# Waits and order of the transposes in a linear-attention stage of a two-block transformer

## The chip, the cores and the metric

The kernel runs as one program on one core of a Trainium2 chip. The metric is the device time of one execution in microseconds (us). The numbers below come from three timed runs and one profiled execution of the kernel before. Engines are called by their short names: PE (TensorE, matmuls and transposes), PEld (its weight loads), ACT (ScalarE), DVE (VectorE), POOL (GpSimd), SP (SyncE, which issues the loads).

## The reference, cut to what matters

Two transformer blocks run one after the other on 512 tokens of width 1024. The second block's mixer is gated linear attention with 4 heads, key width 128 and value width 256, run forward and backward over chunks of 64 tokens. Only that mixer is touched. Its core:

```
def gla_chunked(q, k, v, log_a, s0):
    q = q * (K ** -0.5)
    b = jnp.cumsum(log_a, axis=3)
    b_mid = b[:, :, :, CHUNK // 2 - 1:CHUNK // 2, :]
    b_last = b[:, :, :, CHUNK - 1:, :]
    scores = jnp.einsum('bhnik,bhnjk->bhnij', q * jnp.exp(b - b_mid), k * jnp.exp(b_mid - b))
    scores = jnp.where(causal, scores, 0.0)
    o_intra = jnp.einsum('bhnij,bhnjv->bhniv', scores, v)
    kv = jnp.einsum('bhnjk,bhnjv->nbhkv', k * jnp.exp(b_last - b), v)
    decay = jnp.moveaxis(jnp.exp(b_last[:, :, :, 0, :]), 2, 0)
    s_final, s_before = lax.scan(step, s0, (decay, kv))      # s <- decay * s + kv
    o_inter = jnp.einsum('bhnik,nbhkv->bhniv', q * jnp.exp(b), s_before)
    return o_intra + o_inter, s_final

o = rmsnorm(o, g_head)            # per head, over its 256 values
y_gla = (o * jax.nn.silu(g)) @ w_gla_out
```

log_a is log_sigmoid of a low-rank projection z plus a bias, divided by 16. The inputs q, k, v, g are products of the normed tokens with one wide matrix.

## The kernel before

Every fp32 product is made from three matmuls on split operands (high x high, low x high, high x low). A **tile** is one column block of 128 outputs for all 512 tokens: 8 k-blocks x 3 matmuls of 128x512 (line 1921), into PSUM bank G[0] or G[1]. Its weights pass through raw (DMA), whi (ACT, `high_part`, line 462) and wlo (DVE, `low_part`, line 468), two buffers of each.

The linear attention stage is in `gla_pe`, `gla_act` and `gla_dve`. It walks over eight **units** u = 0 to 7: head h = u // 2, direction r = u % 2. In the gaps between the attention's matmuls PE works on the tiles m, m+1, m+2 of the next head (or, from tile 24 on, of the convolution), in half tiles of 12 matmuls. No scheduler is at work: each engine runs its instructions in the order in which these functions write them, and semaphores (`g_...`) hold them back.

What happens in a unit:

- `z(u+1)` writes the next unit's decay logits into PSUM bank X[3]. ACT's `decay` reads the bank (Abs, then Exp and Ln, lines 2480 to 2484, semaphore g_ln), then DVE's `decay` reads it once (line 2606) and goes on in SBUF: subtract (701), scan (2611 or 2613), two differences and a copy, and then raises g_sums (line 2623). ACT's `exps` turns that into five exponentials, DVE's `factors` multiplies them by k and q and raises g_ke.
- `scores(u)` writes X[2]; DVE's `mask(u)` (2642) copies it under the causal mask into Am; `intra(u)` multiplies it by the values into the output banks AD and MS.
- `outer(u, n)` for n = 0 to 3 makes the k v products of two chunks in X[0] and X[1]; DVE's `states(u, n)` (2657) adds them to the running state and raises g_kv_taken, without which `outer(u, n+1)` waits; `inter(u, n)` multiplies the state by q.
- **Turns** are groups of four 128x128 transposes into the same bank X[3]: `turn_v` (the next head's values, in units with r = 1, two halves, 2352), `turn_o` (the previous head's output, in units with r = 0 and h > 0, two halves, 2374) and `turn_ke` (at the end of each unit, 2363). ACT copies v and ke out (2503, 2499). For the output, ACT's `scale_o` takes the mean square and scales AD and MS into oN (2535 to 2540, semaphore g_on), the turn follows, DVE's `gate_o` (2663) multiplies it by the gate into tb[3], ACT's `high` (2545) and DVE's `low_o` (2668) split it.

Since X[3] is shared, a turn may only write it when the decay's logits have been read. Before, the first `turn_v` and the first `turn_o` of a unit wait for g_sums, which comes at the end of DVE's `decay`.

`conv(n)` is four DVE operations on the convolution (2678 to 2689) for the odd tiles from 25 on, so in units 6 and 7 only.

Of the kernel before, what the change touches and what calls it, by code (L numbers as in the profile page):

```python
# [136 lines left out]
def program(nc, A, out, scr):  # L137
# [3 lines left out]
    def S(name):  # L141
        if name not in sems:
            sems[name] = ctx.enter_context(nc.semaphore(name))
        return sems[name]
# [4 lines left out]
    with ctx:  # L149
# [2173 lines left out]
        def gla_pe(E):  # L2323
            p = E.eng

            def tile(n, lo=0, hi=KD, parts=False):
                j = n % 2
                if lo == 0:
                    E.eng.wait_ge(S(f"free_G{j}"), USE0["hd"] + n // 2 + 1)
                    E.eng.wait_ge(S("w_split"), TILE0["hd"] + n + 3)  # L2330
                for kk in range(lo, hi):
                    if parts:
                        E.eng.wait_ge(S("part_ready"), E.nth("part_ready"))
                    mm = three(E, j, G[j][:, :], Ahi, Alo, kk, kk == 0, kk == KD - 1)
                if hi == KD:
                    mm.then_inc(S("tile_done"), 1)
# [7 lines left out]

            def turn_v(h, half):
                if half == 0:
                    E.eng.wait_ge(S("g_sums"), 1 if h == 0 else 2 * h + 1)
                else:
                    E.eng.wait_ge(S("g_v_copied"), 2 * h + 1)
                E.eng.wait_ge(S("g_v"), 2 * h + half + 1)  # L2350
                for b in range(4):
                    mm = p.transpose(X[3][:, b * P:(b + 1) * P], vT[:, half, b * P:(b + 1) * P], ident)
                mm.then_inc(S("g_v_turned"), 1)
# [12 lines left out]
            def turn_o(h, half):  # L2366
                if half == 0:
                    E.eng.wait_ge(S("g_on"), h + 1)
                    if h < GH - 1:
                        E.eng.wait_ge(S("g_sums"), 2 * h + 4)  # L2370
                else:
                    E.eng.wait_ge(S("g_o_taken"), 2 * h + 1)
                for b in range(4):
                    mm = p.transpose(X[3][:, b * P:(b + 1) * P], oN[:, b, half * P:(half + 1) * P], ident)
                mm.then_inc(S("g_o_turned"), 1)
# [60 lines left out]
            for u in range(NU):  # L2436
                h, r = u // 2, u % 2
                m = 6 * (h + 1) + 3 * r
                tile(m, 0, 4)
                if u + 1 < NU:  # L2440
                    z(u + 1)
                tile(m, 4, KD)
                if r == 0 and h > 0:
                    turn_o(h - 1, 0)
                scores(u)
                if r == 1 and h + 1 < GH:
                    turn_v(h + 1, 0)
                outer(u, 0)
                tile(m + 1, 0, 4)
                intra(u)  # L2450
                if r == 0 and h > 0:
                    turn_o(h - 1, 1)
                if r == 1 and h + 1 < GH:
                    turn_v(h + 1, 1)
                outer(u, 1)
                inter(u, 0)
                tile(m + 1, 4, KD)
                outer(u, 2)
                inter(u, 1)
                tile(m + 2, 0, 4)  # L2460
                outer(u, 3)
                inter(u, 2)
                tile(m + 2, 4, KD)
                inter(u, 3)
                if u + 1 < NU:
                    turn_ke(u + 1)
# [7 lines left out]
        def gla_act(E):  # L2474
# [90 lines left out]
            for u in range(NU):  # L2565
                h, r = u // 2, u % 2
                m = 6 * (h + 1) + 3 * r
                if u + 1 < NU:
                    decay(u + 1)
                if r == 0 and h > 0:  # L2570
                    scale_o(h - 1)
                take(m)
                if u + 1 < NU:
                    exps(u + 1)
                if r == 0 and h > 0:
                    high(h - 1, 0)
                    high(h - 1, 1)
                if r == 1 and h + 1 < GH:
                    copy_v(h + 1, 0)
                    copy_v(h + 1, 1)  # L2580
                take(m + 1)
                take(m + 2)
                if r == 1 and h + 1 < GH:
                    log_exp(E)
                if u + 1 < NU:
                    copy_ke(u + 1)
# [8 lines left out]
        def gla_dve(E):  # L2595
# [7 lines left out]
            def decay(u):  # L2603
                h, r = u // 2, u % 2
                E.eng.wait_ge(S("g_ln"), u + 1)
                v.tensor_scalar(tb[1][:, :], X[3][:, :], vec[:, V_BDEC + 4 * r + h:V_BDEC + 4 * r + h + 1], 0.0,
                                ALU.add, ALU.min)
                v.drain()
                each(E, (tb[1][:, :], tb[1][:, :], tb[0][:, :], ALU.subtract))
                if r == 0:  # L2610
                    v.tensor_tensor_scan(tb[2][:, :], con[:, C_CF:C_CF + T], tb[1][:, :], 0.0, ALU.mult, ALU.add)
                else:
                    v.tensor_tensor_scan(tb[2][:, ::-1], con[:, C_CB:C_CB + T][:, ::-1], tb[1][:, ::-1], 0.0,
                                         ALU.mult, ALU.add)
                v.drain()
                mid, end = (31, 63) if r == 0 else (32, 0)
                sh = [P, 8, CHUNK]
                v.tensor_tensor(tb[1].rearrange("p (c t) -> p c t", t=CHUNK),
                                b3[:, :, end:end + 1].to_broadcast(sh), b3, ALU.subtract)
                v.tensor_tensor(tb[0].rearrange("p (c t) -> p c t", t=CHUNK), b3,  # L2620
                                b3[:, :, mid:mid + 1].to_broadcast(sh), ALU.subtract)
                v.tensor_copy(dsum[:, :], b3[:, :, end])
                v.drain().then_inc(S("g_sums"), 1)
# [78 lines left out]
            for u in range(NU):  # L2702
                h, r = u // 2, u % 2
                m = 6 * (h + 1) + 3 * r
                if u + 1 < NU:
                    decay(u + 1)
                low(m)
                conv(m)
                if r == 0 and h > 0:
                    gate_o(h - 1, 0)  # L2710
                mask(u)
                states(u, 0)
                if u + 1 < NU:
                    factors(u + 1)
                if r == 0 and h > 0:
                    low_o(h - 1, 0)
                    gate_o(h - 1, 1)
                states(u, 1)
                if r == 0 and h > 0:
                    low_o(h - 1, 1)  # L2720
                low(m + 1)
                conv(m + 1)
                states(u, 2)
                states(u, 3)
                low(m + 2)
                conv(m + 2)
# [236 lines left out]
```

## Time and profile before

| | us |
|---|---|
| median of 3 runs | 2476.98 |
| lowest and highest | 2474.41, 2478.2 |
| the profiled execution's own time | 2477.59 |
| its span in the trace | 2475.8 |
| PE busy in the span | 2287.5 (92%) |
| DVE busy | 1066.9 (43%) |
| ACT busy | 843.8 (34%) |
| mean granted TensorE clock | 0.962 of full |

The eight units run from about 1474 to 1742 us of the span, some 11% of it. A busy PE is not always at full rate: the trace also has the clock granted to it, as a share of the full 2.4 GHz (0.50 is the lower of its two levels, 1.2 GHz).

Three views are used. The **stretches** view gives, per stretch start:end of the span, its length, the busy us (and instructions) of PE, PEld, DVE, ACT, POOL, then the mean granted TensorE clock, the busy share of the DMA engines and GB/s. The **waits** view says who waited for whom: us in total, times, the longest. The **timeline** gives start us, duration us, engine, line, operation, out<-in, and in brackets how long the engine sat idle before it and what released it. DVEq is an instruction of DVE's sequencer, here a drain that raises a semaphore. Matmuls overlap, so a row's duration is longer than the step to the next row.

### The profile page before, as it was taken

Reading aid. Unit: us, or ns where it says so; the run is one execution under the profiler, and the core shown is the slowest. Engines: PE = TensorE matmul, PEld = TensorE weight load, DVE = VectorE, ACT = ScalarE, POOL = GpSimd, SP = SyncE. Lnnn points to the kernel's source line nnn. Section 1 sums busy time; section 2 is a strip of 40 time slices with the busy share of each in tenths; the row PEclk is TensorE's granted clock in tenths of the full one; section 3 lists DMA queues with packets and bytes.
Section 4 is the critical chain, followed back from the end, with each engine's and each line's share of the span. In section 5 each row is a group of like instructions: output and inputs, shape, how many; then the busy total and the mean of one; then the engine's idle time right before and its main releaser. Section 6 shows DMA issues by size and latency. Waiting matters only on the chain.

```text
span 2475.8 us, 29368 instructions
## 1 busy us (share of the span) xinstructions
PE 2287.5 (92%) x11126; PEld 1741.5 (70%) x11126; DVE 1066.9 (43%) x1591; ACT 843.8 (34%) x1288; POOL 39.7 (2%) x29
## 2 busy tenths in 40 slices
PE   4588899999998789999999999998999998999997
PEld 2354667777866556888888766666888876888885
DVE  4685343323346664534334344444433334333332
ACT  4332332222235464433223344333222223222222
POOL 3200000000000000000000000000000000000000
PEclk9698899999999899999999999989999999999998
DMA  6589545545422003233233211111333322332331
GB/s 187 192 272 306 199 136 181 179 149 186 141 76 69 9 18 95 71 109 104 83 106 115 70 51 52 51 40 47 88 100 93 93 85 68 93 111 85 94 106 55
DMA packets 360892, 269.98 MB, mean 109 GB/s; under 512 B 20402, under 2 KB 346400, under 8 KB 350544
## 3 DMA queue, kind: packets, MB, share of 16 engines
q1 hardware_dynamic: 346928, 256.37, 33.8%
q10 hardware_dynamic: 13856, 12.13, 1.9%
q8 instruction: 73, 1.20, 0.2%
q14 instruction: 35, 0.29, 0.0%
HBM read 265.39 MB, written 3.08 MB: 108 GB/s over the span
## 4 chain that ended last, share of the span: by engine, by line
PE 80%; DVE 7%; ACT 4%; DVEq 2%; issue 2%; DMA 2%; POOLq 2%; ACTq 1%; SPq 0%; POOL 0%
PE G L482 58%; PE G L1921 8%; PE AD L394 2%; DVE tb L562 1%; PE MS L1257 1%; PE MS L2150 1%; PE X L2131 1%; PE X L2397 1%; ACT whi L462 1%; PE X L1663 1%; DVE wlo L468 1%; DVEq L561 1%; PE X L1627 1%; DMA TTall<-blocks 0%; PE G L1123 0%
## 5 line engine op out<-in xcount | busy, mean ns | idle before, releaser
L468 DVE TENSOR_TENSOR wlo<-raw,whi 128x1024 fp32r<-128x1024 f32 (+1 forms) x296 | 380.8, 1287 | 1010.0 <-ACT whi L462 1009.0
L462 ACT ACTIVATE whi<-raw 128x1024 fp32r<-128x1024 f32 (+1 forms) x296 | 328.1, 1108 | 940.7 <-PE G L482 778.7
L482 PE MATMUL G<-Ahi,whi 128*128 128x512 f32 x1440 | 574.8, 399 | 17.0 <-DVE Alo L567 9.7
L482 PE MATMUL G<-Ahi,wlo 128*128 128x512 f32 x1440 | 563.6, 391 | 0.0
L482 PE MATMUL G<-Alo,whi 128*128 128x512 f32 x1440 | 563.6, 391 | 0.0
L482 PEld LDWEIGHTS G<-Ahi,whi 128*128 128x128 f32 x1440 | 272.3, 189 | 99.2 <-issue 30.6
L482 PEld LDWEIGHTS G<-Ahi,wlo 128*128 128x128 f32 x1440 | 272.6, 189 | 58.2 <-issue 3.4
L482 PEld LDWEIGHTS G<-Alo,whi 128*128 128x128 f32 x1440 | 272.2, 189 | 57.8
L482 PE MATMUL G<-mhi,whi 128*128 128x512 f32 x528 | 212.0, 402 | 0.0
L482 PE MATMUL G<-mlo,whi 128*128 128x512 f32 x528 | 205.7, 390 | 0.0
L482 PE MATMUL G<-mhi,wlo 128*128 128x512 f32 x528 | 205.5, 389 | 0.0
L1921 PE MATMUL G<-Ahi,whi 128*128 128x512 f32 x320 | 135.8, 424 | 5.2 <-DVE Alo L567 3.8
L1921 PE MATMUL G<-Ahi,wlo 128*128 128x512 f32 x320 | 128.7, 402 | 0.0
L1921 PE MATMUL G<-Alo,whi 128*128 128x512 f32 x320 | 128.0, 400 | 0.0
L482 PEld LDWEIGHTS G<-mhi,whi 128*128 128x128 f32 x528 | 99.1, 188 | 26.7 <-issue 7.0
L482 PEld LDWEIGHTS G<-mhi,wlo 128*128 128x128 f32 x528 | 99.2, 188 | 23.1 <-issue 3.1
L482 PEld LDWEIGHTS G<-mlo,whi 128*128 128x128 f32 x528 | 99.1, 188 | 21.1
L1322 ACT ACTIVATE mhi<-tb 128x512 fp32r<-128x512 f32 (+1 forms) x66 | 41.7, 632 | 149.4 <-DVEq L1349 149.4
L1921 PEld LDWEIGHTS G<-Ahi,whi 128*128 128x128 f32 x320 | 62.4, 195 | 39.1 <-issue 21.6
L1921 PEld LDWEIGHTS G<-Alo,whi 128*128 128x128 f32 x320 | 62.5, 195 | 14.2
L1263 ACT ACTIVATE sq<-xT 128x512 f32 (+1 forms) x48 | 30.3, 632 | 119.1 <-DVEq L1366 87.6
L1921 PEld LDWEIGHTS G<-Ahi,wlo 128*128 128x128 f32 x320 | 62.6, 196 | 11.3
(503 smaller groups left out, 2673.1 us busy)
## 6 DMA issues: line engine op xcount, KB each, us to landing
ada_s<-in_ada_w SPq DMA_DIRECT2D x48, 1024.0 KB, 7.5
raw<-in_w_in SPq DMA_DIRECT2D x64, 512.0 KB, 4.1
ada_ff<-in_w_ada SPq DMA_DIRECT2D x24, 1024.0 KB, 6.1
raw<-in_ffn_w_gate SPq DMA_DIRECT2D x44, 512.0 KB, 3.9
raw<-in_ffn_w_up SPq DMA_DIRECT2D x44, 512.0 KB, 3.9
raw<-in_ffn_w_down SPq DMA_DIRECT2D x32, 704.0 KB, 4.7
raw<-in_w_ffn_in SPq DMA_DIRECT2D x44, 512.0 KB, 3.9
raw<-in_w_ffn_out SPq DMA_DIRECT2D x16, 704.0 KB, 4.7
```

The costliest lines, as they stand in the source:

```text
L394: mm = E.eng.matmul(AD[32 * b:32 * b + n, :], cv, buf[:, b * 512:(b + 1) * 512], start=k == 0, stop=k == KD - 1)
L462: last = E.eng.activation(whi[j][:, k0:k0 + k, 0:c], raw[j][:, k0:k0 + k, 0:c], ACT.Copy)
L468: last = E.eng.tensor_tensor(wlo[j][:, k0:k0 + k, 0:c], raw[j][:, k0:k0 + k, 0:c], whi[j][:, k0:k0 + k, 0:c].bitcast(FP32), ALU.subtract)
L482: mm = E.eng.matmul(out_, a[j][:, k0 + kk, 0:c], b(kk), start=first and kk == 0 and n == 0, stop=last and kk == k - 1 and n == 2)
L561: E.eng.drain()
L562: E.eng.scalar_tensor_tensor(tb[k % 2][:, 0:n], src(k), a(k), rstd[:, 0:n], ALU.mult, ALU.mult)\
L1257: E.eng.matmul(MS[:, :], ones, sq[j][:, :], start=first, stop=last).then_inc(S("sq_free"), 1)
L1263: E.eng.activation(sq[j][:, :], xT[:, bass.ds(n, 1), :].rearrange("p o t -> p (o t)"), ACT.Square)\
L1322: E.eng.activation(mhi[:, bass.ds(u, 1), :].rearrange("p o t -> p (o t)"), tb[1][:, :], ACT.Copy)\
L1627: mm = E.eng.matmul(out_, w[a][:, kk, :], b[:, kk, :], start=first and m == 0, stop=last and m == 2)
L1663: mm = E.eng.matmul(X[1][:, a * GV:(a + 1) * GV], x[:, kk, a * P:(a + 1) * P], y[:, kk, :], start=kk == 0 and m == 0, stop=kk == KD - 1 an ...
L1921: mm = E.eng.matmul(out_, a[j][:, kk, :], b[:, kk, :], start=first and n == 0, stop=last and n == 2)
```

## The change

- **Semaphore.** DVE raises a new semaphore g_z_taken after its first operation of `decay`, the one that reads X[3]. The first `turn_v` and the first `turn_o` of a unit wait for it where they waited for g_sums. No instruction is added for that: the drain that raises it was there.
- **PE, units with r = 0 and h > 0.** `turn_o(h-1, 0)` moves from ahead of `scores(u)` to behind the first half of tile m+1; `turn_o(h-1, 1)` moves from behind `intra(u)` to behind the second half of tile m+1.
- **ACT, the same units.** `scale_o(h-1)` moves ahead of `decay(u+1)`; `high(h-1, 0)` ahead of `exps(u+1)`; `high(h-1, 1)` behind `take(m+1)`.
- **DVE, units with r = 0.** `mask(u)` and `states(u, 0)` move to the front, ahead of `decay(u+1)`; `gate_o(h-1, 0)` ahead of `low(m)`; `states(u, 1)` and `states(u, 2)` ahead of `factors(u+1)`. In units with r = 1 only `conv(m)` moves, behind `states(u, 1)`.

```
--- before.py
+++ after.py
@@ -2344,7 +2344,7 @@
             def turn_v(h, half):
                 if half == 0:
-                    E.eng.wait_ge(S("g_sums"), 1 if h == 0 else 2 * h + 1)
+                    E.eng.wait_ge(S("g_z_taken"), 2 * h + 1)
                 else:
                     E.eng.wait_ge(S("g_v_copied"), 2 * h + 1)
                 E.eng.wait_ge(S("g_v"), 2 * h + half + 1)
@@ -2367,7 +2367,7 @@
                 if half == 0:
                     E.eng.wait_ge(S("g_on"), h + 1)
                     if h < GH - 1:
-                        E.eng.wait_ge(S("g_sums"), 2 * h + 4)
+                        E.eng.wait_ge(S("g_z_taken"), 2 * h + 4)
                 else:
                     E.eng.wait_ge(S("g_o_taken"), 2 * h + 1)
                 for b in range(4):
@@ -2440,21 +2440,21 @@
                 if u + 1 < NU:
                     z(u + 1)
                 tile(m, 4, KD)
-                if r == 0 and h > 0:
-                    turn_o(h - 1, 0)
                 scores(u)
                 if r == 1 and h + 1 < GH:
                     turn_v(h + 1, 0)
                 outer(u, 0)
                 tile(m + 1, 0, 4)
+                if r == 0 and h > 0:
+                    turn_o(h - 1, 0)
                 intra(u)
-                if r == 0 and h > 0:
-                    turn_o(h - 1, 1)
                 if r == 1 and h + 1 < GH:
                     turn_v(h + 1, 1)
                 outer(u, 1)
                 inter(u, 0)
                 tile(m + 1, 4, KD)
+                if r == 0 and h > 0:
+                    turn_o(h - 1, 1)
                 outer(u, 2)
                 inter(u, 1)
                 tile(m + 2, 0, 4)
@@ -2565,20 +2565,21 @@
             for u in range(NU):
                 h, r = u // 2, u % 2
                 m = 6 * (h + 1) + 3 * r
+                if r == 0 and h > 0:
+                    scale_o(h - 1)
                 if u + 1 < NU:
                     decay(u + 1)
+                take(m)
                 if r == 0 and h > 0:
-                    scale_o(h - 1)
-                take(m)
+                    high(h - 1, 0)
                 if u + 1 < NU:
                     exps(u + 1)
-                if r == 0 and h > 0:
-                    high(h - 1, 0)
-                    high(h - 1, 1)
                 if r == 1 and h + 1 < GH:
                     copy_v(h + 1, 0)
                     copy_v(h + 1, 1)
                 take(m + 1)
+                if r == 0 and h > 0:
+                    high(h - 1, 1)
                 take(m + 2)
                 if r == 1 and h + 1 < GH:
                     log_exp(E)
@@ -2605,7 +2606,7 @@
                 E.eng.wait_ge(S("g_ln"), u + 1)
                 v.tensor_scalar(tb[1][:, :], X[3][:, :], vec[:, V_BDEC + 4 * r + h:V_BDEC + 4 * r + h + 1], 0.0,
                                 ALU.add, ALU.min)
-                v.drain()
+                v.drain().then_inc(S("g_z_taken"), 1)
                 each(E, (tb[1][:, :], tb[1][:, :], tb[0][:, :], ALU.subtract))
                 if r == 0:
                     v.tensor_tensor_scan(tb[2][:, :], con[:, C_CF:C_CF + T], tb[1][:, :], 0.0, ALU.mult, ALU.add)
@@ -2702,25 +2703,34 @@
             for u in range(NU):
                 h, r = u // 2, u % 2
                 m = 6 * (h + 1) + 3 * r
+                if r == 0:
+                    mask(u)
+                    states(u, 0)
                 if u + 1 < NU:
                     decay(u + 1)
-                low(m)
-                conv(m)
                 if r == 0 and h > 0:
                     gate_o(h - 1, 0)
-                mask(u)
-                states(u, 0)
+                low(m)
+                if r == 1:
+                    mask(u)
+                    states(u, 0)
+                if r == 0:
+                    states(u, 1)
+                    if h > 0:
+                        low_o(h - 1, 0)
+                        gate_o(h - 1, 1)
+                    states(u, 2)
                 if u + 1 < NU:
                     factors(u + 1)
-                if r == 0 and h > 0:
-                    low_o(h - 1, 0)
-                    gate_o(h - 1, 1)
-                states(u, 1)
+                if r == 1:
+                    states(u, 1)
+                conv(m)
                 if r == 0 and h > 0:
                     low_o(h - 1, 1)
                 low(m + 1)
                 conv(m + 1)
-                states(u, 2)
+                if r == 1:
+                    states(u, 2)
                 states(u, 3)
                 low(m + 2)
                 conv(m + 2)
```

PE, unit 2 (the first with a turned output), from the end of tile 12 (its G matmuls) on. The change takes the turn away ahead of the scores (X<-qd,kh and X<-qd,kd):

```order
 L1921 MATMUL G<-Ahi,wlo 128x512
 L1921 MATMUL G<-Alo,whi 128x512
-L2374 MATMUL X<-con,oN 128x128 x4
 L2382 MATMUL X<-qd,kh 128x2x32
 L2382 MATMUL X<-qd,kd 128x2x32
```

and puts it behind the first half of tile 13, ahead of intra (AD<-vN,Am and MS<-vN,Am), where the second turn leaves as well:

```order
 L1921 MATMUL G<-Ahi,wlo 128x512
 L1921 MATMUL G<-Alo,whi 128x512
+L2374 MATMUL X<-con,oN 128x128 x4
 L2406 MATMUL AD<-vN,Am 128x256 x2
 L2406 MATMUL MS<-vN,Am 128x256 x2
-L2374 MATMUL X<-con,oN 128x128 x4
 L2397 MATMUL X<-vN,sq 128x256 x2
```

What moved: the first turn stands eight score matmuls, one outer pair and a half tile later.

ACT, the same unit, from the copy of ke (sq<-X) to the Exp of exps (sq<-tb). The first fence is the kernel before, the second the change:

```order
L2499 ACTIVATE sq<-X 128x512
L2480 ACTIVATE tb<-X,vec 128x512
L2482 ACTIVATE tb<-tb 128x512
L2484 ACTIVATE tb<-tb,con 128x512
L2535 ACTIVATE oN,oms<-AD 128x256 x2
L2535 ACTIVATE oN,oms<-MS 128x256 x2
L1845 ACTIVATE oms<-oms,epsb 128x4
L1847 ACTIVATE oms<-oms 128x4
L2540 ACTIVATE oN<-AD,oms 128x256 x2
L2540 ACTIVATE oN<-MS,oms 128x256 x2
L462 ACTIVATE whi<-raw 128x1024
```

```order
L2535 ACTIVATE oN,oms<-AD 128x256 x2
L2535 ACTIVATE oN,oms<-MS 128x256 x2
L1845 ACTIVATE oms<-oms,epsb 128x4
L1847 ACTIVATE oms<-oms 128x4
L2540 ACTIVATE oN<-AD,oms 128x256 x2
L2540 ACTIVATE oN<-MS,oms 128x256 x2
L2480 ACTIVATE tb<-X,vec 128x512
L2482 ACTIVATE tb<-tb 128x512
L2484 ACTIVATE tb<-tb,con 128x512
L462 ACTIVATE whi<-raw 128x1024
L2519 ACTIVATE kT<-G 128x512
L2545 ACTIVATE Chi<-tb 128x512
```

What moved: the eight rows of scale_o stand ahead of the three of decay, and one high (Chi<-tb) ahead of exps.

DVE, the same unit, from the end of the decay (the copy dsum<-tb) on; before it stood behind low(m-1), now behind mask and states. The change:

```order
L2623 COPY dsum<-tb 128x8
L2664 SCALAR_TENSOR_TENSOR tb<-X,vec,gS 128x512
L468 TENSOR_TENSOR wlo<-raw,whi 128x1024
L2658 SCALAR_TENSOR_TENSOR rstd<-raw,dec,X 128x256
L2658 SCALAR_TENSOR_TENSOR rstd<-rstd,dec,X 128x256
L2669 TENSOR_TENSOR Clo<-tb,Chi 128x512
L2664 SCALAR_TENSOR_TENSOR tb<-X,vec,gS 128x512
L2658 SCALAR_TENSOR_TENSOR raw<-rstd,dec,X 128x256
L2658 SCALAR_TENSOR_TENSOR raw<-raw,dec,X 128x256
L2632 MEMSET kh 128x8x32
```

and the kernel before, from the same copy on:

```order
L2622 COPY dsum<-tb 128x8
L468 TENSOR_TENSOR wlo<-raw,whi 128x1024
L2663 SCALAR_TENSOR_TENSOR tb<-X,vec,gS 128x512
L2642 COPY_PREDICATED Am<-con,X 128x512
L2657 SCALAR_TENSOR_TENSOR raw<-S,dec,X 128x256
L2657 SCALAR_TENSOR_TENSOR raw<-raw,dec,X 128x256
L2631 MEMSET kh 128x8x32
```

What moved: the first gate (tb<-X,vec,gS) stands ahead of the weight split, and the states 1 and 2 and the second gate ahead of the factors (from the memset of kh on).

## Rows read from the trace of the kernel before

**Rows 1.** Stretches view: units 0, 1, 2, 4, 5 and 6, each from turn_ke to turn_ke.
```profile
1474.35:1502.76 28.41, 27.69 (x135) 19.04 (x133) 14.42 (x23) 11.32 (x17) 0.00 (x0) 1.00 0.21 57
1502.76:1534.86 32.10, 30.13 (x144) 21.24 (x142) 14.44 (x23) 12.11 (x19) 0.00 (x0) 0.95 0.19 50
1534.86:1571.95 37.09, 33.30 (x144) 23.81 (x142) 17.35 (x27) 15.53 (x33) 0.00 (x0) 0.86 0.16 43
...
1604.08:1640.90 36.82, 32.68 (x144) 23.39 (x143) 17.36 (x27) 15.51 (x33) 0.00 (x0) 0.86 0.16 43
1640.90:1674.48 33.58, 31.61 (x144) 22.12 (x143) 14.55 (x23) 12.15 (x19) 0.00 (x0) 0.90 0.20 48
1674.48:1712.59 38.11, 31.84 (x145) 22.57 (x143) 20.01 (x31) 14.98 (x32) 0.00 (x0) 0.91 0.17 42
```

**Rows 2.** Waits view of PE, 1440 to 1800 us.
```profile
PE X L2374 <- DVEq L2623: 11.7, 3, 4.1
PE X L2352 <- DVEq L2623: 5.9, 3, 2.0
PE X L2397 <- DVEq L2659: 2.5, 1, 2.5
...
PE AD L2406 <- DVE Am L2642: 1.2, 2, 0.9
PE X L2342 <- ACT sq L2499: 0.4, 1, 0.4
```

**Rows 3.** Timeline of PE, units 0 and 1.
```profile
1483.78 0.70 PE L2397 MATMUL X<-vN,sq 64*128 64x256 f32 x4
...
1487.78 1.13 PE L2406 MATMUL AD<-vN,Am 128*128 128x256 f32 x4 [0.35 <-DVE Am L2642]
...
1506.11 1.12 PE L2342 MATMUL X<-ddT,wdec 32*128 32x512 f32 x2
...
1510.02 0.33 PE L2382 MATMUL X<-qd,kh 128*128 128x64 f32 x2
...
1513.88 0.66 PE L2352 MATMUL X<-con,vT 128*128 128x128 f32 x4 [1.97 <-DVEq L2623]
```

**Rows 4.** Timeline of DVE, unit 1.
```profile
1509.52 0.75 DVE L2606 TENSOR_SCALAR tb<-X,vec 128x512 f32<-128x512 f32 x1 [4.91 <-ACTq L2485]
...
1513.91 1.23 DVE L468 TENSOR_TENSOR wlo<-raw,whi 128x1024 fp32r<-128x1024 f32 x1
1515.06 0.74 DVE L2642 COPY_PREDICATED Am<-con,X 128x512 f32<-128x512 int32 x1
1515.69 0.46 DVE L2657 SCALAR_TENSOR_TENSOR raw<-S,dec,X 128x256 f32<-128x256 f32 x1
...
1517.05 0.27 DVE L2629 MEMSET kh<- 128x256 f32 x1 [0.30 <-issue]
...
1519.75 0.29 DVE L2635 COPY kh<-kd 128x256 f32<-128x256 f32 x1
```

**Rows 5.** Timeline of ACT, unit 2: decay, scale_o, then whi.
```profile
1539.41 0.69 ACT L2480 ACTIVATE tb<-X,vec 128x512 f32<-128x512 f32 x1 [1.53 <-PE X L2342]
...
1541.70 0.38 ACT L2535 ACTIVATE oN<-AD 128x256 f32<-128x256 f32 x1
...
1545.41 1.07 ACT L462 ACTIVATE whi<-raw 128x1024 fp32r<-128x1024 f32 x1
```

**Rows 6.** Timeline of PE, unit 2: the first turn_o.
```profile
1546.11 1.09 PE L2374 MATMUL X<-con,oN 128*128 128x128 f32 x4 [3.79 <-DVEq L2623]
```

**Rows 7.** Stretches view of PE alone, units 1 and 6.
```profile
1517.00:1519.00 2.00, 2.00 (x6) 0.56 0.77 228
...
1706.00:1708.00 2.00, 0.18 (x2) 1.00 0.59 179
```

**Rows 8.** Timeline of DVE, unit 6: first conv row, next state.
```profile
1703.45 0.68 DVE L2678 TENSOR_TENSOR cvs<-cvs,G 128x512 f32<-128x512 f32 x1
...
1706.57 0.48 DVE L2657 SCALAR_TENSOR_TENSOR raw<-rstd,dec,X 128x256 f32<-128x256 f32 x1
```

More of the change, by code:

```diff
@@ L2346, in turn_v @@
                 if half == 0:
-                    E.eng.wait_ge(S("g_sums"), 1 if h == 0 else 2 * h + 1)
+                    E.eng.wait_ge(S("g_z_taken"), 2 * h + 1)
                 else:
@@ L2369, in turn_o @@
                     if h < GH - 1:
-                        E.eng.wait_ge(S("g_sums"), 2 * h + 4)
+                        E.eng.wait_ge(S("g_z_taken"), 2 * h + 4)
                 else:
@@ L2442, in gla_pe @@
                 tile(m, 4, KD)
-                if r == 0 and h > 0:
-                    turn_o(h - 1, 0)
                 scores(u)
@@ L2449, in gla_pe @@
                 tile(m + 1, 0, 4)
+                if r == 0 and h > 0:
+                    turn_o(h - 1, 0)
                 intra(u)
-                if r == 0 and h > 0:
-                    turn_o(h - 1, 1)
                 if r == 1 and h + 1 < GH:
@@ L2457, in gla_pe @@
                 tile(m + 1, 4, KD)
+                if r == 0 and h > 0:
+                    turn_o(h - 1, 1)
                 outer(u, 2)
@@ L2567, in gla_act @@
                 m = 6 * (h + 1) + 3 * r
+                if r == 0 and h > 0:
+                    scale_o(h - 1)
                 if u + 1 < NU:
                     decay(u + 1)
+                take(m)
                 if r == 0 and h > 0:
-                    scale_o(h - 1)
-                take(m)
+                    high(h - 1, 0)
                 if u + 1 < NU:
                     exps(u + 1)
-                if r == 0 and h > 0:
-                    high(h - 1, 0)
-                    high(h - 1, 1)
                 if r == 1 and h + 1 < GH:
@@ L2581, in gla_act @@
                 take(m + 1)
+                if r == 0 and h > 0:
+                    high(h - 1, 1)
                 take(m + 2)
@@ L2607, in decay @@
                                 ALU.add, ALU.min)
-                v.drain()
+                v.drain().then_inc(S("g_z_taken"), 1)
                 each(E, (tb[1][:, :], tb[1][:, :], tb[0][:, :], ALU.subtract))
@@ L2704, in gla_dve @@
                 m = 6 * (h + 1) + 3 * r
+                if r == 0:
+                    mask(u)
+                    states(u, 0)
                 if u + 1 < NU:
                     decay(u + 1)
-                low(m)
-                conv(m)
                 if r == 0 and h > 0:
                     gate_o(h - 1, 0)
-                mask(u)
-                states(u, 0)
+                low(m)
+                if r == 1:
+                    mask(u)
+                    states(u, 0)
+                if r == 0:
+                    states(u, 1)
+                    if h > 0:
+                        low_o(h - 1, 0)
+                        gate_o(h - 1, 1)
+                    states(u, 2)
                 if u + 1 < NU:
                     factors(u + 1)
[L2715 to L2718, printed above, removed]
+                if r == 1:
+                    states(u, 1)
+                conv(m)
                 if r == 0 and h > 0:
@@ L2722, in gla_dve @@
                 conv(m + 1)
-                states(u, 2)
+                if r == 1:
+                    states(u, 2)
                 states(u, 3)
```

## Prediction

> **What bounds the kernel now.** PE does. I read the stretches view first, over the eight units from one turn_ke to the next [rows 1]. The reader should compare lengths. The units hold the same tiles: those with r = 1 and a next head have exactly unit 1's work, those with r = 0 and h > 0 (2, 4, 6) the same again, and unit 0 lacks only the two turns. Yet unit 0 takes 28.41 us at clock 1.00, units 1 and 3 take 32.1 (unit 3 repeats unit 1's row), unit 5 33.58, and units 2, 4, 6 take 37.09, 36.82 and 38.11 at 0.86 to 0.91. So some 4 to 9 us of each are not work. DVE and ACT are busy for 12 to 20 us of each, so neither is short of throughput; what counts is the order in their queues.
>
> The waits view then names what is lost [rows 2]: three first turns of o wait 11.7 us in all and three first turns of v 5.9 us, both for DVE's drain at line 2623, that is for g_sums. Beside them stand one wait of 2.5 us for a state (unit 6), two for the mask (0.35 in unit 0 [rows 3] and 0.9 in unit 7), and 0.4 of a z in unit 0.
>
> Waiting is only half of it: 3 x 2.0 and 3 x 3.9 are 17.6 us, while the lengths hold about twice as much. The timeline shows unit 1's turn at 1513.88 after 1.97 us idle [rows 3], and the stretch behind it runs at clock 0.56, close to the lower level of 1.2 GHz [rows 7]. Each of the six waits is followed by such a piece (mean clocks 0.95, 0.86, 0.86, 0.90, 0.91), unit 0 without a long wait has none [rows 1].
>
> **The nominal unit.** Unit 0: 28.41 less its waits of 0.4 and 0.35 is 27.7. Two turns more, at 0.6 each (the row of four shows 0.66, the tail of the last included [rows 3]), make 28.9 us for a unit without waits at the full clock.
>
> **The semaphore, units with r = 1.** The first read of X[3] by DVE takes 0.75 us of the 4.39 from 1509.52 to 1513.91 [rows 4]. In unit 1 g_z_taken comes at about 1510.4. The scores end at 1513.88 - 1.97 = 1511.91 [rows 3], so the turn starts there and its wait is gone. What is late next? `intra` needs the mask. It would start at 1511.91 + 0.6 (turn) + 3.65 (outer and half tile, 1487.78 - 0.35 - 1483.78 in unit 0 [rows 3]) = 1516.2; the mask, which this unit does not move, ends at 1515.06 + 0.74 = 1515.8 [rows 4]. A slack of 0.4 us: no wait. So units 1 and 3 fall from 32.1 to 28.9 (3.2 each) and unit 5 from 33.58 (4.7).
>
> **The move, units with r = 0 and a previous head.** I lay out unit 2.
> - PE. turn_ke is at 1534.86 [rows 1]; z is 3.35 later as in unit 1 (1506.11 - 1502.76), at 1538.2; the scores 3.91 after that, at 1542.1, and last 1.89, to 1544.0 [rows 3]. With no turn ahead of them nothing waits. Outer and half tile, 3.65, bring the first turn_o to 1547.65.
> - ACT is free at 1539.41 - 1.53 = 1537.9. scale_o lasts 1545.41 - 1541.70 = 3.7, so oN is ready at 1541.6; decay lasts 2.3, so g_ln comes at 1543.9, 2.2 us later than before [rows 5]. That costs nothing as long as DVE is then at its mask.
> - DVE takes mask (0.63) at 1544.1, states 0 (1515.69 to 1517.05, 1.36), and reaches the decay at 1546.1; its read of the bank ends at 1546.9 [rows 4]. The turn_o comes at 1547.65: slack 0.8. Before, this turn started at 1546.11 after 3.79 us idle [rows 6].
> - On DVE there follow the rest of decay (to 1550.5), gate_o (taken as 0.7, the form is that of the mask's 0.74), low(m) 1.15 to 1552.3, states 1 to 1553.7 [rows 4]. PE is at the end of its unit at 1534.86 + 28.9 = 1563.8; counted back by inter 0.6, two half tiles of 2.95 (3.65 less the outer's 0.70) and two outer-inter pairs of 1.3 (estimated from that 0.70), outer 2 starts at 1554.7, 1.0 after its state. The second turn_o stands just ahead of it and finds the first gate long done (1551.2).
> - Then second gate to 1555.4, states 2 to 1556.8 (needed at 1558.9), factors 3.0 (1517.05 to 1520.04 [rows 4]) to 1559.8 (needed by turn_ke at 1563.8), low_o and low(m+1) to 1561.7, states 3 to 1562.3 (needed at 1563.2, slack 0.9). ACT has the first `high` at 1551.9 and exps some 2.7 later, ahead of the factors. The loads that SP issues wait for low(m) and low(m+1), which come some 5 us later than before; the engines that move them are busy 0.16 to 0.21 of the time [rows 1] and the tile they serve is more than a unit's half away, so I cost that at nothing; were that cover gone, a split would wait for its load.
>
> So units 2 and 4 fall to 28.9: 8.2 and 7.9 us.
>
> **Unit 6.** Its conv of tile 25 takes 1706.57 - 1703.45 = 3.1 us on DVE [rows 8]. Before, it stood ahead of states 2 and made the 2.5 us wait [rows 2]. The change puts states 2 ahead of it, but states 3 is still behind: 1562.3 + 3.1 = 1565.4 in unit 2's times, against 1563.2. So a wait of about 2.2 us remains, one place further on. Bounds: 0 if PE gets there late anyway, 2.6 if DVE is as late as its slacks allow. After such a wait the clock need not fall: after the 2.48 us at 1707.8 it stood at 1.00 [rows 7]. I take 28.9 + 2.3 = 31.2, a gain of 6.9.
>
> **Units 0 and 7.** In unit 0 the mask now precedes decay, so 0.35 goes; factors come later behind states 2, with 4 us to spare. In unit 7 conv(27) no longer precedes the mask, so 0.9 goes.
>
> **The sum.** 2 x 3.2 + 4.7 + 8.2 + 7.9 + 6.9 + 0.35 + 0.9 = 35.3 us. Against the profiled execution's own 2477.6 us (1.8 above its span) that is 2442.3. The median of the runs shown is 0.6 lower, which gives 2441.7; I say 2442. The stages before and after are PE's and unchanged.
>
> **Where a page speaks against it.** First the rows: of the 35.3 us, 17.6 are waits and about 16 are slow clock (per unit length less nominal less waits: 1.2, 1.2, 2.7, 4.4, 3.8, 2.9). Unit 0, where the scores are followed by outer with no idle time, has clock 1.00, and it begins with four transposes [rows 1]. The Trainium skill (TensorE: Matmul & The Clock Gate, Part 4: PE-mode transpose) says that transposes do not bring the full clock about as matmuls do. In the units with r = 1 the turn of v still follows right behind the small score matmuls, so by that rule the lower clock could come there without an idle time. By the trace so far the idle time is what all six have in common. I keep it as a rival.
>
> **Rivals.**
> - *The slow clock stays though the waits go.* If it stays behind scores and turn in units 1, 3, 5 only, 5.1 us come back: 2447. If in all six, 16.2: 2458. For it: the 2.5 us wait behind a half tile did not lower the clock while the 2.0 us waits behind the scores did, so what comes before matters. Against it: unit 0. Chance 0.12.
> - *A new wait takes the old one's place in units 2, 4, 6.* DVE's queue is now one chain from scores through mask, states, decay, gate, split, state. The slacks above are 0.8, 1.0, 0.9 us. If the chain runs 1.5 us later than summed, each of three places waits about 0.6 per unit, 5 us in all, with 2 to 4 us of slow clock on top: 2447 to 2452. Chance 0.14.
> - *The change does not do what it says:* the drain behind the first operation raises the semaphore no earlier than the decay's end. Then the first turn_o waits from 1547.65 to 1550.5, 2.9 us instead of 3.9, and the turn of v as before: about 3 x 1 + 1.25 plus a little clock, 2472. The 0.75 us row of that operation speaks against it [rows 4]. Chance 0.02.
> - *Slower than before: ACT stands in its queue behind the turn.* The first `high` is now ahead of exps and waits for a gate that waits for PE's turn, and the factors and turn_ke hang on exps. The cover is 1563.8 - 1559.8 = 4.0 us. It costs from the point at which the gate comes over 4 us later than I have it, and the whole is slower than before only if it comes about 4 + 35.3 / 3 = 16 us late in each of the three units: at 18 us late, 2477.6 - 35.3 + 3 x 14 = 2484. Only a low granted clock through the whole unit could do that. Chance 0.02.
>
> **How the numbers follow.** The forecast has 0.70: 2442, with its own range from 2438 (no wait left in unit 6, a nominal unit 0.2 shorter) to 2445 (a few tenths of wait in each unit). The range has to hold 8 in 10: 0.70 plus the r = 1 clock case and most of the new waits give 2438 to 2455. A measurement of this kernel can tell about 0.2%, 5 us, from no change. Every case but the last two lies over 5 us below: faster 0.97 (the case at 2472 is just outside 5 us too), same 0.01, slower 0.02.
>
> **What would show it right or wrong.** In the changed profile no PE wait at the turns of v or o for a DVE drain; the units 1 to 5 each 28.9 us long at clock 1.00; a wait of about 2.3 us of PE's inter (line 2416) for a state in unit 6. I am wrong if PE waits at outer 2, outer 3 or inter 3 in units 2 and 4, or if the clock of units 1, 3, 5 stays below 0.98 without a wait. If the lengths are right and the time is not, the difference is outside of the stage, where I expect none.

## The result and the profile after

The changed kernel takes 2440.65 us (median of 4 runs, 2439.65 to 2441.91), the kernel before 2477.59 us beside it (2474.41 to 2479.38). The ratio is 0.9846 with a 95% interval of 0.9827 to 0.9866: 36.9 us or 1.5% faster. The profiled execution took 2441.41 us. Every median here and below is over executions with a mean granted clock of 0.96 to 0.97; one of the six of state_first_again ran at 0.83, took 2628.2 us and is left out.

The page's head and PE's row (busy us, share of the span, instructions):

```profile
span 2439.6 us, 29369 instructions
...
PE 2268.1 (93%) x11126; PEld 1726.8 (71%) x11126; DVE 1067.0 (44%) x1591; ACT 844.1 (35%) x1288; POOL 39.9 (2%) x29
```

The stretches view of the seven units from turn_ke to turn_ke, with the columns of [rows 1]:

```profile
1475.22:1503.02 27.80, 27.43 (x135) 19.11 (x134) 14.42 (x23) 11.33 (x17) 0.00 (x0) 1.00 0.17 46
1503.02:1531.58 28.56, 28.56 (x144) 19.94 (x143) 14.44 (x23) 12.18 (x19) 0.00 (x0) 1.00 0.25 68
1531.58:1559.91 28.33, 28.33 (x145) 20.07 (x143) 17.20 (x27) 15.32 (x33) 0.00 (x0) 1.00 0.15 40
1559.91:1588.49 28.58, 28.58 (x144) 19.94 (x142) 14.45 (x23) 12.16 (x19) 0.00 (x0) 1.00 0.26 72
1588.49:1616.81 28.32, 28.32 (x144) 20.06 (x142) 17.19 (x27) 15.32 (x33) 0.00 (x0) 1.00 0.14 39
1616.81:1645.37 28.56, 28.56 (x144) 19.95 (x142) 14.44 (x23) 12.17 (x19) 0.00 (x0) 1.00 0.29 73
1645.37:1676.90 31.53, 28.62 (x144) 20.07 (x142) 20.54 (x32) 15.98 (x33) 0.00 (x0) 0.99 0.20 51
```

Compare lengths and clocks with [rows 1]. The units 1 to 5 are now within 0.3 us of each other at clock 1.00. From turn_ke(0) to turn_ke(7) it was 238.24 us (1474.35 to 1712.59) and is 201.68 us (1475.22 to 1676.90): 36.6 us, which is the whole gain of 36.2 us in the span. The rest of the program took 0.9 us ahead of turn_ke(0) and gave 0.5 us behind turn_ke(7).

The waits of PE in the stage, where [rows 2] had 11.7, 5.9, 2.5, 1.2 and 0.4 us:

```profile
PE MS L2416 <- DVEq L2659: 2.9, 1, 2.9
PE G L1921 <- DVE wlo L468: 1.5, 1, 1.5
PE X L2342 <- ACT sq L2499: 0.4, 1, 0.4
```

The waits of turns and masks are gone. One of 2.9 us at an inter has come. The 1.5 us stand at a tile's first matmul at 1463.7 us, ahead of the units; the kernel before has 1.4 us there, so they are none of the change's. The 0.4 us are as they were.

The timeline of unit 2: PE at z, at the first score and at the first turn of o; DVE from the mask to the decay's read of the bank (2607), the next row, the decay's last row (2623), and the first gate (2664); ACT at scale_o, decay and whi. They answer to [rows 4 to 6].

```profile
1534.93 1.12 PE L2342 MATMUL X<-ddT,wdec 32*128 32x512 f32 x2
...
1538.83 0.33 PE L2382 MATMUL X<-qd,kh 128*128 128x64 f32 x2
...
1544.15 0.60 PE L2374 MATMUL X<-con,oN 128*128 128x128 f32 x4
```

```profile
1540.76 0.74 DVE L2643 COPY_PREDICATED Am<-con,X 128x512 f32<-128x512 int32 x1 [7.34 <-PE X L2382]
...
1542.73 0.75 DVE L2607 TENSOR_SCALAR tb<-X,vec 128x512 f32<-128x512 f32 x1 [0.22 <-issue]
1543.61 0.69 DVE L701 TENSOR_TENSOR tb<-tb 128x512 f32<-128x512 f32 x1
...
1546.89 0.17 DVE L2623 COPY dsum<-tb 128x8 f32<-128x8 f32 x1
1547.18 0.75 DVE L2664 SCALAR_TENSOR_TENSOR tb<-X,vec,gS 128x512 f32<-128x512 f32 x1
```

```profile
1534.46 0.38 ACT L2535 ACTIVATE oN<-AD 128x256 f32<-128x256 f32 x1
...
1538.18 0.71 ACT L2480 ACTIVATE tb<-X,vec 128x512 f32<-128x512 f32 x1
...
1540.54 1.06 ACT L462 ACTIVATE whi<-raw 128x1024 fp32r<-128x1024 f32 x1 [0.16 <-issue]
```

The turn starts at 1544.15 with no idle time in brackets. The scaled output was there at 1538.2, six us earlier, and the bank was read at 1542.73 + 0.75 = 1543.5, only 0.7 us earlier. The decay that the turn would have waited for before ends at 1547.1, 2.9 us after the turn's start.

### The profile page after: what moved, and what is told of

It is laid out like the page before. It is cut to its first block, busy times and chain, and to the rows that moved or that the text cites. A ratio compares the mean times of both kernels' runs of the same rounds, so it can differ in the third digit from the quotient of the medians.

```text
span 2439.6 us, 29369 instructions
## 1 busy us (share of the span) xinstructions
PE 2268.1 (93%) x11126; PEld 1726.8 (71%) x11126; DVE 1067.0 (44%) x1591; ACT 844.1 (35%) x1288; POOL 39.9 (2%) x29
## 4 chain that ended last, share of the span: by engine, by line
PE 81%; DVE 7%; ACT 3%; DVEq 2%; issue 2%; DMA 2%; POOLq 2%; ACTq 1%; SPq 0%; POOL 0%
PE G L482 58%; PE G L1921 9%; PE AD L394 2%; DVE tb L562 1%; PE MS L1257 1%; PE MS L2150 1%; PE X L2131 1%; PE X L2397 1%; PE X L1663 1%; DVE wlo L468 1%; DVEq L561 1%; DMA ada_s<-in_ada_w 1%; ACT whi L462 1%; PE X L1627 1%; DVEq L702 1%
## 5 line engine op out<-in xcount | busy, mean ns | idle before, releaser
L482 PEld LDWEIGHTS G<-Ahi,whi 128*128 128x128 f32 x1440 | 271.9, 189 | 99.4 <-issue 30.6
L482 PEld LDWEIGHTS G<-Ahi,wlo 128*128 128x128 f32 x1440 | 271.9, 189 | 58.2 <-issue 3.4
L1921 PEld LDWEIGHTS G<-Ahi,whi 128*128 128x128 f32 x320 | 60.3, 188 | 36.9 <-issue 20.1
L1353 DVE TENSOR_TENSOR mlo<-tb,mhi 128x512 fp32r<-128x512 f32 (+1 forms) x66 | 45.7, 693 | 52.4 <-ACT mhi L1322 52.4
```

Source lines behind the costliest of these rows:

```text
L482: mm = E.eng.matmul(out_, a[j][:, k0 + kk, 0:c], b(kk), start=first and kk == 0 and n == 0, stop=last and kk == k - 1 and n == 2)
L1353: E.eng.tensor_tensor(mlo[:, bass.ds(u, 1), :].rearrange("p o t -> p (o t)"), tb[1][:, :], mhi[:, bass.ds(u, 1), :].rearrange("p o t -> p ...
L1921: mm = E.eng.matmul(out_, a[j][:, kk, :], b[:, kk, :], start=first and n == 0, stop=last and n == 2)
```

## The experiments

Units are compared by their lengths in the stretches view, since the time of the whole program scatters by several us from one execution to the next (2473.2 to 2482.6 in ten of the kernel before), for reasons outside of this stage too: turn_ke(0) alone lies between 1469.8 and 1477.7 us in these profiles. Each kernel has one profile. The changed kernel has two, and their units 0 to 5 agree within 0.02 us. Times are medians. Each kernel ran beside the kernel before on the same chip: that one took 2477.1 us beside sem_only, moves_only, v_waits_sums and state_first, 2475.6 beside v_filled, scale_late and mask_late, and 2475.8 beside second_early, dve_plus, after_again and state_first_again. "Slow clock" below is what a unit is longer than in the changed kernel (28.6 us with turns of v, 28.3 with turns of o) less its waits.

**The semaphore alone.** The kernel before, all orders as they were:

```
-                v.drain()
+                v.drain().then_inc(S("g_z_taken"), 1)
                 each(E, (tb[1][:, :], tb[1][:, :], tb[0][:, :], ALU.subtract))
 (and the waits of turn_v and turn_o as in the change)
```

> The kernel before with the new semaphore alone: turns wait for DVE's read of the bank, every order as it was. My theory: units 1, 3, 5 lose their wait and the slow clock behind it and fall to 28.6 us each as in the changed kernel (3.5 + 3.5 + 5.0 = 12 us). In units 2, 4, 6 the first turn of o is then released by scale_o, about 0.5 us earlier than by the sums, and waits 3.3 us instead of 3.8 to 4.1; the slow clock behind it stays. In all about 13.5 us: 2464 us. Rival (the semaphore is the change, the order adds little): about 2445 us.

2462.8 us (2458.1 to 2465.0), 14.3 below the kernel before. The waits view and the stretches of units 1, 2, 4 and 6:

```profile
PE X L2374 <- ACT oN L2540: 9.9, 3, 3.3
```

```profile
1504.47:1533.09 28.62, 28.62 (x145) 19.95 (x143) 14.45 (x23) 12.17 (x19) 0.00 (x0) 1.00 0.21 56
1533.09:1566.48 33.39, 30.10 (x144) 20.96 (x143) 17.26 (x27) 15.52 (x33) 0.00 (x0) 0.95 0.18 48
1595.08:1630.04 34.96, 31.67 (x144) 22.25 (x143) 17.35 (x27) 15.52 (x33) 0.00 (x0) 0.90 0.17 46
1658.62:1698.99 40.37, 34.60 (x144) 24.28 (x142) 20.02 (x31) 14.98 (x32) 0.00 (x0) 0.83 0.16 40
```

Units with r = 1 are done with, 28.6 us each. In the others the releaser has changed its name from the sums to scale_o (oN, line 2540) and the wait is 3.3 us instead of 3.9. Two releasers stood nearly at the same time, so removing one gives almost nothing. The same 3.3 us of waiting was followed by very different amounts of slow clock: unit 2 is 5.1 us over the 28.3 that it has in the changed kernel, unit 4 6.6, unit 6 12.0. That is 1.8 and 3.3 us of slow clock, and 6.2 in unit 6, where a second wait of 2.5 us for a state stands as well.

**The order alone.** The changed kernel with the old waits:

```
-                    E.eng.wait_ge(S("g_z_taken"), 2 * h + 1)
+                    E.eng.wait_ge(S("g_sums"), 1 if h == 0 else 2 * h + 1)
...
-                        E.eng.wait_ge(S("g_z_taken"), 2 * h + 4)
+                        E.eng.wait_ge(S("g_sums"), 2 * h + 4)
```

> The changed kernel with both turns waiting for the end of the decay's sums again: the order alone. My theory: in units 2, 4, 6 the first turn of o now comes 2 us later on PE but the sums come later too (DVE does mask and states first), so it waits about 3.0 us, with some 1 to 1.5 us of slow clock behind it; units 1, 3, 5 are as long as before the change (32.1, 32.1, 33.6). Together 24 to 26 us above the changed kernel: 2465 us. Rival (the order gives the gain of the r = 0 units by itself): 12 us above, 2453 us.

2463.2 us (2459.6 to 2471.1 in seven executions; the profiled one took 2468.3, so the lengths below are at the high end). Waits and unit 2:

```profile
PE X L2374 <- DVEq L2624: 9.2, 3, 3.3
PE X L2352 <- DVEq L2624: 6.1, 3, 2.0
```

```profile
1535.52:1569.84 34.32, 31.39 (x145) 21.73 (x143) 17.29 (x27) 15.30 (x33) 0.00 (x0) 0.90 0.12 33
```

The waits are as expected: 9.2 us in three waits for the sums (line 2624), though the turn comes later, because DVE's decay comes later too. The slow clock in this profile is more than the 1 to 1.5 us that I had given each: 3.0 in unit 2, 1.8 in unit 4. Apart the two halves of the change give 14.3 and 13.9 us, together 36.9. Neither is most of it. By the unit lengths the semaphore alone gives the whole gain of the units 1, 3 and 5 (12.0 of 12.1 us); in the units 2, 4 and 6 the semaphore alone gives 3.3, the order alone 7.1, and only both together 23.8 us.

**One kind of wait put back.** The changed kernel, with only

```
-                    E.eng.wait_ge(S("g_z_taken"), 2 * h + 1)
+                    E.eng.wait_ge(S("g_sums"), 1 if h == 0 else 2 * h + 1)
```

in turn_v.

> The changed kernel in which only the turn of v waits for the sums again, in units 1, 3, 5. It restores three waits of 2.0 us. My theory: each brings slow clock back with it, so the time rises by 12 us to 2453 us, and the lengths of the three units are 32.1, 32.1 and 32 to 34. Rival (a wait costs its own length, the slow clock has another cause): 5.9 us, 2446.6 us.

2449.7 us (2449.0 to 2450.8), 9 us above the changed kernel, between the two theories. Units 1, 3 and 5:

```profile
1501.95:1534.08 32.13, 30.11 (x145) 21.02 (x143) 14.56 (x23) 12.16 (x19) 0.00 (x0) 0.95 0.22 60
1562.40:1594.57 32.17, 30.15 (x145) 21.21 (x143) 14.44 (x23) 12.17 (x19) 0.00 (x0) 0.95 0.23 64
1622.88:1653.46 30.58, 28.56 (x145) 20.10 (x143) 14.45 (x23) 12.17 (x19) 0.00 (x0) 1.00 0.27 69
```

Three equal waits of 2.0 us: two brought 1.6 us of slow clock, the third none (30.58 = 28.56 + 2.02). My expectation that each brings it was wrong by that third. Counting the same waits of 2.0 us in the kernel before and in moves_only, eight of nine were followed by slow clock.

**PE kept at work while it waits.** The same kernel with

```
                 if r == 1 and h + 1 < GH:
+                    E.eng.wait_ge(S("g_kv_taken"), 4 * u)
+                    for _ in range(8):
+                        p.matmul(X[0][:, :], Ahi[:, 0, 0:P], Ahi[:, 0, :], start=True, stop=True)
                     turn_v(h + 1, 0)
```

> The kernel v_waits_sums with eight matmuls of 128x512 (1.8 us, result not used) ahead of the turn of v in units 1, 3, 5, so that PE works while it would wait for the sums. My theory: slow clock follows idle time, so the units keep clock 1.00 and are 28.6 + 2.0 = 30.6 us long, 6 us above the changed kernel: 2446.7 us, less than v_waits_sums (2449.7) though PE does more. Rival (the small score matmuls and the transposes bring the slow clock, with or without idle time): the clock of the three units stays at 0.90 to 0.95 and the time at 2449 to 2453 us.

2443.8 us (2443.1 to 2447.2): 31.8 below its kernel before, where the kernel without the filling is 27.4 below its own. The 95% intervals of the two ratios just overlap (0.9856 to 0.9888 and 0.9875 to 0.9909), so the units carry the argument. The added matmuls of unit 1, then units 1, 3 and 5:

```profile
1510.57 2.10 PE L2447 MATMUL X<-Ahi 128*128 128x512 f32 x8
```

```profile
1501.62:1532.19 30.57, 30.46 (x152) 21.45 (x151) 14.43 (x23) 12.15 (x19) 0.00 (x0) 1.00 0.23 63
1560.52:1591.08 30.56, 30.45 (x152) 21.44 (x150) 14.45 (x23) 12.15 (x19) 0.00 (x0) 1.00 0.24 67
1619.45:1650.03 30.58, 30.47 (x152) 21.44 (x151) 14.43 (x23) 12.15 (x19) 0.00 (x0) 1.00 0.28 69
```

More work and less time: units 1 and 3 are 1.6 us shorter than in v_waits_sums, unit 5 is the same. The lengths are 30.6 as expected and the clock is 1.00 in all three. The turn still starts only when the sums are there, so the wait's own 2.0 us stay; what goes is the slow clock. The small score matmuls and the transposes are not enough to bring it: here they stand around the added matmuls, in the changed kernel right behind each other, and the clock is 1.00 in both. So it took PE's idle time to bring it. The filling was tried for the turns of v alone; that it would do the same at the longer waits for the turns of o is not shown.

**ACT's order put back.** The changed kernel with scale_o behind decay:

```
-                if r == 0 and h > 0:
-                    scale_o(h - 1)
                 if u + 1 < NU:
                     decay(u + 1)
+                if r == 0 and h > 0:
+                    scale_o(h - 1)
```

> The changed kernel with ACT's scale_o behind the decay again. In unit 2 of the changed kernel ACT is free at 1534.5 us, z is at 1534.9 and the first turn of o at 1544.15. My theory: decay first gives its end at about 1538.4 and the scaled output at 1542.1, still 2 us ahead of the turn; DVE reaches its decay at 1542.7 in any case. So nothing changes: 2440.7 us, units 2 and 4 at 28.3 us. Rival (the outputs must be scaled first for the later turn to find them): PE waits for scale_o, 1 to 3 us per unit with slow clock behind it, 2445 to 2455 us.

2440.1 us (2437.2 to 2443.5); units 2 and 4:

```profile
1529.30:1557.63 28.33, 28.33 (x144) 20.08 (x143) 17.20 (x27) 15.44 (x33) 0.00 (x0) 1.00 0.15 39
1586.22:1614.58 28.36, 28.36 (x144) 20.06 (x142) 17.18 (x27) 15.42 (x33) 0.00 (x0) 1.00 0.14 39
```

No difference. Scaling the outputs ahead of the decay is worth nothing once their turn is a half tile later.

**DVE's order put back at the front.** Mask and states 0 behind decay, gate and low in units with r = 0:

```
-                if r == 0:
-                    mask(u)
-                    states(u, 0)
                 if u + 1 < NU:
                     decay(u + 1)
                 if r == 0 and h > 0:
                     gate_o(h - 1, 0)
                 low(m)
-                if r == 1:
-                    mask(u)
-                    states(u, 0)
+                mask(u)
+                states(u, 0)
```

> The changed kernel in which DVE does the mask and the first states behind decay, gate and low in units with r = 0, as in the kernel before; PE's and ACT's orders as changed. My theory: gate waits for the turn, the split and the mask stand behind it, so PE waits about 2.7 us for the mask at intra in units 2, 4, 6, with 0 to 3 us of slow clock each: about 2451 us. Rival (the order on PE is what counts, DVE has time enough): 2441 to 2443 us.

2454.3 us (2451.0 to 2454.8), 3 us above what I expected. PE's wait for the mask and unit 2:

```profile
PE AD L2406 <- DVE Am L2643: 8.8, 4, 3.0
```

```profile
1526.86:1559.79 32.93, 30.23 (x145) 21.08 (x143) 17.12 (x27) 15.31 (x33) 0.00 (x0) 0.95 0.12 34
```

One of the four waits is unit 0's, as in [rows 3]; each of the other three is 2.8 us on average, and units 2 and 4 (33.28 us) have about 2 us of slow clock on top. The move on PE needs this one on DVE: the gate waits for a turn that is now late, and what stands behind the gate is late with it.

**The second turn put back** behind intra, all else as changed:

```
                 intra(u)
+                if r == 0 and h > 0:
+                    turn_o(h - 1, 1)
...
                 tile(m + 1, 4, KD)
-                if r == 0 and h > 0:
-                    turn_o(h - 1, 1)
```

> The changed kernel with only the second turn of o back at its old place behind intra. My theory: the first gate ends at 1547.85 us in unit 2 of the changed kernel and the turn would be due at 1546.4, so PE waits about 1.4 us in units 2, 4, 6, 4.3 us in all: 2445 us. Rival (the second move is for nothing, the gate is in time): 2441 us.

2447.9 us (2446.5 to 2449.5). The turns in units 2 and 4, and the two units:

```profile
1549.65 0.66 PE L2374 MATMUL X<-con,oN 128*128 128x128 f32 x4 [1.50 <-DVE tb L2664]
...
1608.61 0.66 PE L2374 MATMUL X<-con,oN 128*128 128x128 f32 x4 [1.86 <-DVE tb L2664]
```

```profile
1533.25:1563.30 30.05, 28.55 (x145) 20.00 (x143) 17.36 (x27) 15.30 (x33) 0.00 (x0) 1.00 0.14 37
1591.87:1623.82 31.95, 30.09 (x145) 20.88 (x143) 17.36 (x27) 15.30 (x33) 0.00 (x0) 0.95 0.14 36
```

The wait is 1.5 us in units 2 and 6, about as expected, and no slow clock came behind it. In unit 4 it is 1.86 us, and 1.8 us of slow clock came with it (31.95), which I had not priced.

**The slack of DVE's chain.** Two operations more ahead of the decay in units 2, 4, 6:

```
                     states(u, 0)
+                    if h > 0:
+                        for _ in range(2):
+                            v.tensor_tensor(tb[3][:, :], con[:, C_CF:C_CF + T], con[:, C_CB:C_CB + T], ALU.mult)
+                            v.drain()
```

> The changed kernel with two more DVE operations of 0.69 us each and a drain behind each (1.5 us together; their result is not used) ahead of the decay in units 2, 4, 6. It probes the slack of the chain mask, states, decay. My theory: the read of the bank ended 0.6 us ahead of the turn, so the turn waits about 0.9 us; the places further on have slack enough, but unit 6's last inter is 1.5 us later: 0.9 + 0.9 + 1.5 = 3.3 us, 2444 us, and waits as short as these bring no slow clock. Rival (the slacks are used up at three places, each with slow clock behind): 2447 to 2452 us.

2443.3 us (2438.7 to 2445.2). The first turn and unit 2:

```profile
1541.25 0.63 PE L2374 MATMUL X<-con,oN 128*128 128x128 f32 x4 [0.90 <-DVEq L2609]
```

```profile
1527.63:1557.04 29.41, 28.51 (x145) 19.99 (x143) 18.56 (x29) 15.30 (x33) 0.00 (x0) 1.00 0.14 37
```

1.5 us more on DVE cost 0.9 us at the turn (so the slack is 0.6) and 29.41 - 28.33 = 1.1 in the unit, at clock 1.00. Unit 6 is longer by the same 1.1 (32.38 against 31.31 us in after_again), so nothing piled up further on.

**A version that is faster still.** In unit 6 the last state stands behind the conv. The changed kernel's PE and DVE there (2679 is the conv's first row, 2658 the state), and the stretch behind:

```profile
1676.09 0.44 PE L2416 MATMUL MS<-raw,qi 128*64 128x256 f32 x1 [2.90 <-DVEq L2659]
```

```profile
1671.98 0.68 DVE L2679 TENSOR_TENSOR cvs<-cvs,G 128x512 f32<-128x512 f32 x1
...
1675.53 0.48 DVE L2658 SCALAR_TENSOR_TENSOR rstd<-raw,dec,X 128x256 f32<-128x256 f32 x1
```

```profile
1676.00:1678.00 2.00, 1.91 (x9) 1.30 (x10) 1.23 (x2) 0.00 (x0) 0.00 (x0) 0.59 0.00 0
```

The edit:

```
                 low(m + 1)
-                conv(m + 1)
                 if r == 1:
+                    conv(m + 1)
                     states(u, 2)
                 states(u, 3)
+                if r == 0:
+                    conv(m + 1)
```

> The changed kernel with DVE's last state of units with r = 0 ahead of conv of tile m+1 (only unit 6 has one). My theory: PE's wait of 2.9 us at the last inter of unit 6 goes, and the 1.1 us of slow clock behind it: 2436.7 us, unit 6 is 28.4 us long. Rival (the conv is late for something else, the free G bank or the weight split of tiles 27 and 28, and the wait only moves): 2439 to 2441 us.

2437.9 us (2435.4 to 2439.8), 39.2 below its kernel before. I ran it again beside the changed kernel:

> The changed kernel once more, as the one that state_first_again is compared with on the same chip: about 36 us below the kernel before, 2439 to 2442 us.

> The kernel state_first once more, beside the changed kernel on the same chip. Without PE's wait of 2.9 us in unit 6, and with 0 to 1 us of slow clock less: 3 to 4 us below after_again. Rival (the saved wait is spent elsewhere): within 1 us of it.

2440.2 us and 2435.9 us; against the kernel before 0.9856 (0.9842 to 0.9871) and 0.9834 (0.9822 to 0.9847). The intervals overlap by a hair, but unit 6 shows it, first without and then with the edit:

```profile
1646.54:1677.85 31.31, 28.40 (x145) 20.07 (x143) 20.32 (x32) 15.98 (x33) 0.00 (x0) 1.00 0.20 51
```

```profile
1646.65:1674.98 28.33, 28.33 (x144) 20.07 (x143) 17.79 (x28) 14.90 (x32) 0.00 (x0) 1.00 0.16 39
```

The wait is gone and came back nowhere: 4.3 us less by the medians, 3.0 by the unit. This is the fastest kernel of the study by the medians.

## Why the prediction was right, step by step

I predicted 2442, and 2440.65 was measured. The mechanism held; that the two numbers are so close is partly luck, since two errors cancel. Up to turn_ke(7) the sum had 34.4 us where the profiles show 36.6. For unit 7 it had a gain of 0.9, and from turn_ke(7) to its last inter the unit went from 27.0 to 27.2 us.

- *The nominal unit* of 28.9 us was 0.3 to 0.6 too long: it is 28.56 to 28.58 with turns of v, 28.32 and 28.33 with turns of o. Two terms were mis-sized. Unit 0 without its wait of 0.37 is 27.43 us, not 27.7, so the other wait of 0.35 had cost 0.6. And two turns among other matmuls are not 1.2 but 1.1 us for v (28.56 - 27.43) and 0.9 for o (28.33 - 27.43). Over the units this is 0.3 to 0.6 us each, the 2.1 us that the sum lacked and 0.3 more, which unit 6 took back.
- *Units 1, 3, 5* lost 3.5, 3.6 and 5.0 us against 3.2, 3.2 and 4.7. The turn starts behind the scores and no mask wait took its place, so the slack of 0.4 at intra held.
- *Units 2 and 4* lost 8.8 and 8.5 against 8.2 and 7.9. The layout of unit 2 held almost row by row. I had the turn at 9.4 us behind the z; it is at 1544.15 - 1534.93 = 9.2. The slack at the bank was 0.7 where I had 0.8, and dve_plus measured it as 0.6. That the later g_ln costs nothing was right, and scale_late shows it from the other side.
- *Unit 6* went from 38.11 to 31.53, 6.6 against 6.9. The wait was forecast at its place (inter, for the last state), at 2.2 to 2.3 us, and is 2.90, outside of my bound of 2.6. PE came 0.5 us earlier than laid out (27.8 us behind turn_ke, not 28.3) and the state 0.1 later: the conv took 1675.53 - 1671.98 = 3.55 us, not 3.1 (0.4 more before its second row), but DVE reached it a little earlier. And I let the clock stay up behind the wait, by the one case that I had. That case is read rightly, though the row of [rows 7] lies almost wholly inside the wait; behind it the kernel before has

```profile
1708.00:1710.00 2.00, 2.00 (x12) 1.15 (x13) 0.48 (x1) 0.00 (x0) 0.00 (x0) 1.00 0.00 0
```

  But sem_only has the same wait of 2.5 us with slow clock behind it. Nine profiles have the wait of 2.9 us: five show slow clock behind it (this one, v_waits_sums, v_filled, mask_late and second_early), four do not. Here it runs on into unit 7, which is 27.2 us long where after_again, with the clock up, has 25.8. That is why the 0.9 us of unit 7's mask did not show, though its wait is gone.
- *Half of the gain is clock.* Of the 36.6 us up to turn_ke(7), 17.6 are waits that went and 19.0 are PE's busy time for the same matmuls (217.40 to 198.41 us). That the slow clock would go with the waits was the step I was least sure of. It held, and v_filled shows for the turns of v that it is idle time which brings it.
- *The rivals.* By the rule on transposes in the Trainium skill (TensorE: Matmul & The Clock Gate, Part 4: PE-mode transpose) the units with r = 1 could have kept a low clock; they have 1.00, with four transposes right behind the small score matmuls and four more behind intra. That shows only that so few of them do not lower a clock that is up. "A new wait takes the old one's place" happened in unit 6 only. ACT's queue, the rival for a slower kernel, never came near its point: the first `high` waited 5.9 us and delayed exps, but the turn_ke that ends unit 2 starts at 1559.91 us with no idle time. That the semaphore would come no earlier than the sums is refuted by the turn, which starts at 1544.15 while the decay runs to 1547.1. But I had mispriced that case: moves_only makes the turns wait just so, and it took 2463.2 us where I had put 2472. In its profile the slow clock of the units 2, 4 and 6 is 7.9 us where it was 12.8 before; I had counted on a little.

## What to carry to other kernels

Where two releasers of a wait come close together, price the removal of each with the other in place: here each half of the change gave 14 us and both gave 37, and in the units where the two releasers stood close the halves gave 3 and 7 us and both 24. When a wait is moved on one engine, lay out its partners' queues in absolute times and move with it what stands behind the same event (mask_late: 14 us if not). A wait of PE can cost nearly twice its length (1.97 us of wait, 3.5 us of unit 1), and other matmuls in the place of a 2.0 us wait kept the clock up.

## What the runs showed of the hardware that I had not expected

The same wait is followed by slow clock in one unit and not in the next, with the same instructions around it: 2.0 us of idle time brought 1.6, 1.6 and 0 us in v_waits_sums, 3.3 us brought 1.8 and 3.3 in units 2 and 4 of sem_only, and the 2.9 us at unit 6's last inter brought some in five of nine profiles. The shortest wait with slow clock behind it is the one of 1.86 us in second_early; its two of 1.50 us brought none, nor did the three of 0.9 us in dve_plus. What decides between two equal waits none of these runs shows, and so the cost of a wait that one profile shows is a draw. Whether such waits also make a kernel's times scatter more, these few executions don't tell: v_waits_sums, with three of them, spans 1.9 us in four executions, moves_only, with six, 11.5 in seven, and the changed kernel 2.3 in its first four and 7.2 in the four of after_again.
